# Adding two gated branches: from VectorE to a GpSimd transfer that accumulates

## The reference

```python
y_a = jnp.einsum('bse,ed->bsd', o * jax.nn.silu(r), w_gla_out[l])
u = causal_depthwise_conv(cc * cx, conv_w[l])
y_b = jnp.einsum('bsc,cd->bsd', cb * u, w_conv_out[l])
merged = jax.nn.sigmoid(ga) * y_a + jax.nn.sigmoid(gb) * y_b
x = x + jnp.einsum('bsd,de->bse', merged, w_o[l])
```

## Time and profile before

| | |
|---|---|
| median of 3 runs | 2230.9 us |
| span of the profiled execution | 2229.0 us |
| PE busy | 2217.9 us |
| PEld busy | 1844.9 us |
| DVE busy | 1274.6 us |
| ACT busy | 991.3 us |
| POOL busy | 225.7 us |
| DMA, mean over the span | 200 GB/s |

### The profile page before, as it was taken

How to read it: one execution, slowest core, us unless ns; L and a number is a source line. 1 busy time by engine, 2 the same in 40 slices (tenths; PEclk the granted TensorE clock), 3 DMA queues, 4 the chain that set the end, 5 groups by cost and what they waited for, 6 DMA issues and landing times.

```text
span 2229.0 us, 24387 instructions
## 1 busy us (share of the span) xinstructions
PE 2217.9 (100%) x10314; PEld 1844.9 (83%) x10314; DVE 1274.6 (57%) x1061; ACT 991.3 (44%) x950; POOL 225.7 (10%) x253
## 2 busy tenths in 40 slices
PE   9999999999999999999999999999999999999998
PEld 8888888888888888888888888888888888888886
DVE  6577645545556545555454444554555577786755
ACT  7464654333333443344433433433444455555642
POOL 1023010000000000000000100000100121353201
PEclk9999999999999999999999999999999999999999
DMA  9554556678877766655565555555555756555663
GB/s 321 185 179 162 169 180 199 208 221 224 243 228 231 217 202 199 226 186 191 177 201 188 189 189 189 188 189 189 188 185 194 250 191 196 182 177 176 220 238 117
DMA packets 217100, 444.89 MB, mean 200 GB/s; under 512 B 9316, under 2 KB 10484, under 8 KB 216096
## 3 DMA queue, kind: packets, MB, share of 16 engines
q1 hardware_dynamic: 206976, 411.07, 56.1%
q0 software_dynamic: 9728, 32.18, 6.1%
q10 hardware_dynamic: 288, 0.10, 0.0%
HBM read 427.08 MB, written 12.06 MB: 197 GB/s over the span
## 4 chain that ended last, share of the span: by engine, by line
PE 100%; DVE 0%; POOL 0%; POOLq 0%; ACT 0%; issue 0%
PE acc L1390 31%; PE acc L1391 31%; PE acc L1392 31%; PE side L1400 2%; PE side L1478 1%; PE side L1414 1%; PE side L1450 1%; PE side L1464 1%; PE acc L1405 0%; PE side L1435 0%; PE side L1433 0%; PE side L1434 0%; PE side L1499 0%; PE side L1500 0%; POOL X L657 0%; PE side L1521 0%
## 5 line engine op out<-in xcount | busy, mean ns | idle before, releaser
L954 DVE TENSOR_TENSOR wlo<-raw,whi 128x2048 fp32r<-128x2048 f32 x380 | 892.1, 2348 | 739.3 <-ACT whi L674 739.2
L674 ACT ACTIVATE whi<-raw 128x2048 fp32r<-128x2048 f32 x380 | 727.7, 1915 | 784.9 <-PE acc L1392 762.2
L1390 PE MATMUL acc<-whi,setA_lo 128*128 128x512 f32 x1792 | 700.6, 391 | 0.0
L1392 PE MATMUL acc<-whi,setA_hi 128*128 128x512 f32 x1792 | 697.4, 389 | 0.0
L1391 PE MATMUL acc<-wlo,setA_hi 128*128 128x512 f32 x1792 | 697.4, 389 | 0.0
L1390 PE MATMUL acc<-whi,setB_lo 128*128 128x512 f32 x1280 | 502.9, 393 | 0.0
L1391 PE MATMUL acc<-wlo,setB_hi 128*128 128x512 f32 x1280 | 498.8, 390 | 0.0
L1392 PE MATMUL acc<-whi,setB_hi 128*128 128x512 f32 x1280 | 498.3, 389 | 0.0
L1392 PEld LDWEIGHTS acc<-whi,setA_hi 128*128 128x128 f32 x1792 | 336.4, 188 | 70.1
L1390 PEld LDWEIGHTS acc<-whi,setA_lo 128*128 128x128 f32 x1792 | 336.5, 188 | 69.9 <-DVE setA_lo L985 0.6
L1391 PEld LDWEIGHTS acc<-wlo,setA_hi 128*128 128x128 f32 x1792 | 336.6, 188 | 68.2
(11 more groups left out here) (205 smaller groups left out, 1000.8 us busy)
## 6 DMA issues: line engine op xcount, KB each, us to landing
raw<-in_w_in SPq DMA_DIRECT2D x188, 1024.0 KB, 5.2
raw<-in_w_ffn_up SPq DMA_DIRECT2D x64, 1024.0 KB, 5.3
raw<-in_w_ffn_down SPq DMA_DIRECT2D x64, 1024.0 KB, 5.1
raw<-in_w_gla_out SPq DMA_DIRECT2D x16, 1024.0 KB, 5.2
raw<-in_w_conv_out SPq DMA_DIRECT2D x16, 1024.0 KB, 5.2
raw<-in_w_o SPq DMA_DIRECT2D x16, 1024.0 KB, 5.2
raw<-in_w_out SPq DMA_DIRECT2D x16, 1024.0 KB, 5.2
t_scratch<-t5v POOLq DMA_DIRECT2D x8, 512.0 KB, 7.3
```

Of the source, the lines that this page charges most:

```text
L674: e.activation(whi[r][:, :, :], raw[r][:, :, :], ACT.Copy).then_inc(s_hi, 1)
L954: e.tensor_tensor(wlo[r][:, :, :], raw[r][:, :, :], asf(whi[r][:, :, :]), ALU.subtract).then_inc(s_lo, 1)
L1390: e.matmul(o, xl, whi[r][:, k, :], start=kk == 0, stop=False)
L1392: f = e.matmul(o, xh, whi[r][:, k, :], start=False, stop=kk == 15)
```

## The change

The third DVE instruction of each yb unit goes. In its place POOL, in the same quarter's job "post", waits until the GA part of the unit (unit "ya" j) and the two products are there, and issues one DMA from `GA` (columns of this unit, 128 partitions x 2 x 512 floats, 512 KB) to `tmp` with the accumulate operation add: the transfer reads its destination, adds the source, and writes it back. The transfer raises `s_yb` by 16 when it has landed, and PE waits for 16 (j + 1) in place of j + 1. The whole diff:

```diff
--- before.py
+++ after.py
@@ -619,6 +619,12 @@
                         for i, y in ((1, z1), (2, z2)):
                             e.dma_start(y[i:128, :, :], z[0:128 - i, :, :]).then_inc(s_shift, 16)
                             e.dma_start(y[0:i, 1, :], z[128 - i:128, 0, :]).then_inc(s_shift, 16)
+                    elif job == "post" and UNITS[a][0] == "yb":
+                        j = UNITS[a][1]
+                        e.wait_ge(*evacuated(UI["ya", j]))
+                        e.wait_ge(*evacuated(a))
+                        e.dma_start(tmp_of(a)[:, :, :], GA[:, :, 512 * j:512 * j + 512],
+                                    accum_op=ALU.add).then_inc(s_yb, 16)
                     elif job == "post" and UNITS[a][0] == "up":
                         tm = tmp_of(a)[:, :, :]
                         e.wait_ge(*evacuated(a))
@@ -1086,9 +1092,6 @@
                     e.wait_ge(*tmp_free(u))
                     for t in range(2):
                         e.tensor_tensor(tmp_of(u)[:, t, :], acc[u % 2][t][:, :], GB[:, t, cols], ALU.mult).then_inc(ev, 1)
-                    tm = tmp_of(u)[:, :, :]
-                    e.wait_ge(*evacuated(u))
-                    e.tensor_tensor(tm, tm, GA[:, :, cols], ALU.add).then_inc(s_yb, 1)
                 elif kind in ("wo", "down"):
                     if kind == "wo":
                         e.wait_ge(s_x1, 16)
@@ -1532,7 +1535,7 @@
                         if kind == "r":
                             e.wait_ge(s_rx, 2 * j + 2)
                         elif kind == "yb":
-                            e.wait_ge(s_yb, j + 1)
+                            e.wait_ge(s_yb, 16 * (j + 1))
                         elif kind == "up":
                             e.wait_ge(s_pq, j + 1)
                         else:
```

## The result

| | before | changed |
|---|---|---|
| median of 4 runs, us | 2230.91 (2230.81 to 2230.97) | 2242.91 (2241.24 to 2243.0) |
| span of the profiled execution, us | 2229.0 | 2241.1 |
| the profiled execution's own time, us | not recorded | 2242.88 |

The ratio is 1.0052, with a 95% interval from 1.004 to 1.0064: 12.0 us slower. 2242.3 was forecast.

The account below looks back on a forecast made before the run. TensorE (PE) was taken to bound the kernel, with no slack; three waits of 2.6 us plus one of 3.6 give 11.4, so 2230.9 + 11.4 = 2242.3 us. Range 2232.5 to 2262, the forecast's own 2236 to 2251.

Parts of the forecast that it names:

- That PE's wait is the cost, whole, four times: At the transposes that read tmp, PE waits L - 3.4 us per unit, four times, 11.4 us in all, none regained.
- The removed additions are worth nothing: Four DVE additions, 4.9 us, go; no PE instruction waits for DVE, so the gain is 0.
- The start of the issue, 0.29 us after the products: POOL starts issuing the adding transfer 0.29 us after the second GB product ends, as for the conv stage's shift copy.
- L = 6.0 us: Adding transfer from start of issue to landing: 4.5 copy, 1.3 second read, 0.2 overlap; PE waits 2.6 us per unit.
- +1.0 us in the fourth stage: X1's load pushes weight loads back, so the fourth transfer has half the engines for 2 us: wait 3.6 us.
- The clock at 0: PE's pauses of 2.6 and 3.6 us are shorter than 4.9 us, so the granted clock costs 0.
- The signs named: Wrong if no wait at L1400, landing over 8 us, clock falls, waits for wlo/whi, or waits miss span difference by over 1 us.
- Rival A: The transfer hides: adding costs it nothing, L of 4.5 or less, 4.4 us or less, median 2233 to 2235; chance 0.17.
- rival B: Adding transfer much slower, L of 8.5 or more: 20.4 us, 2251; with clock falls 2255 to 2257; chance 0.23.
- the forecast's own range: Median 2236 to 2251 us, for landing after 4.6 to 8.4 us; chance 0.58.

Follow-up runs that it names:

- the copy: Changed kernel with the four GA-to-tmp transfers as plain copies, without the accumulate operation: 2233.18 us.
- the early load: Changed kernel with the 2 MB load of X1 issued one unit (23 us) earlier: 2242.94 us; second trace 2243.70 us.
- the one-wait kernel: Changed kernel without POOL's wait for the ya part of GA before it issues the adding transfer: 2242.08 us.
- the kernel with half the bytes: Changed kernel with only the first 128 tokens of each unit added by the transfer, the other half by DVE: 2232.39 us.
- the filling: Changed kernel with 16 turns of the identity (1.8 us of PE) put ahead of PE's wait for the sum: 2241.64 us.
- the two filled kernels: Changed kernel with 16 identity turns ahead of PE's wait, without and with X1 loaded one unit earlier: 2241.64 and 2242.21 us.

## Why the prediction was right, point by point

**That PE's wait is the cost, whole, four times.** Shown: with the turns a quarter later the time is that of before; with a second transfer the added wait appears in full.

**The removed additions are worth nothing.** Right. PE's new waits are only the transfers'; and in the kernel with late turns DVE is as much relieved as in the change, at 2230.9.

**The start of the issue, 0.29 us after the products.** Mis-sized: 0.58 measured. The shift copy that I took it from goes through one wait, this one through two; with one it is 0.30.

**L = 6.0 us.** Mis-sized by a little. Measured 5.7, 5.3, 5.5 and 6.6. With the late start, PE's ready time less the start of the issue was 3.1 and not 3.4 us, so the term should have read L - 3.1, and 5.3 to 5.7 gives 2.2 to 2.6 us. The stages were 2.47, 2.05 and 2.32 longer where 2.6 was said. L was put together from 4.5 for a copy and 1.3 for the second stream. Both were off, in opposite directions: the copy of GA lands after 3.5, and the adding is worth 1.9 to 2.1, of which 0.5 is issue. That the three shift transfers queued behind it made the shift copy's 4.4 to 4.6 is likely, but no run parts this from its other shape. The Trainium skill ("Collectives: The Full Stack", section "The bandwidth ceiling: the fold count and why AG ≠ RS ≠ AR") states that a reduce moves at about half the rate of a gather, because it reads two sources. The traces agree roughly: 3.3 us against 1.7 from first packet to last, and 182 and 188 GB/s in slices of the changed kernel where the adding transfer has the engines nearly alone, against 403 for a load. In engine time the adding transfer cost 2.5 times the copy.

```profile
879.00:880.00 1.00, 1.00 (x6) 0.82 (x5) 1.00 (x1) 0.00 (x0) 0.90 (x1) 1.00 1.04 403
...
881.00:882.00 1.00, 1.00 (x6) 0.68 (x4) 0.14 (x1) 0.00 (x0) 0.00 (x0) 1.00 1.09 188
882.00:883.00 1.00, 0.22 (x1) 0.00 (x0) 0.00 (x0) 0.00 (x0) 0.00 (x0) 1.00 1.16 182
```

**+1.0 us in the fourth stage.** 6.6 us in the first trace, about 1.0 above the rest, but the reason given, engines shared with the weight loads that X1 pushed back, explains at most a part. X1's own load had landed at 925.1, 3 us before the transfer's issue. By the trace's semaphore events thirteen of the transfer's 16 completions had come after 5.2 us, as in the other stages, and three came at 5.6, 5.6 and 6.6: single engines were behind, and not all of them. With X1's load in its old place the fourth transfer was late (6.2 to 6.7 us) in five traces of eight, whatever its kind (add, copy, half), and on time (5.3) in three. With the load a unit earlier the third one was late (6.1 and 6.3) in two of three. So the load of X1 seems to have to do with it, but doesn't force it, and one late fourth transfer without it (6.3 us) shows that it is not all. What puts single engines behind stays open.

**The clock at 0.** This step failed. I had read from the end of the span that PE's clock holds for 4.9 us after its last work, and took shorter pauses for safe. That was one pause, seen once. In the first trace of the change a pause of 3.1 us was followed by a fall when PE had already been at work again for 1.0 us. In the four traces of the change and of the early load, pauses of 1.7 to 3.1 us were followed by a fall in 7 cases of 16 (in the change 1 and 2 of four, in the early load 2 and 2); at 0.50 for 3.4 us with PE at work a fall costs 1.6 to 1.7 us. The falls stand behind the longer pauses: seven behind the nine of 2.07 to 3.08 us, none behind the seven of 1.74 to 1.84. The copy had a pause of 2.7 us and the one-wait kernel one of 2.9, both with a fall; the kernel with half the bytes had one of 2.5 us and no fall, and the one with two transfers, with waits of 7.4 to 8.0 us, four falls of four. Waits of up to 1.0 us, with the filling, had none in eight. The runs without a trace point the same way: their mean granted clock is 0.998 or 0.999 in all ten of the two filled kernels, as in the kernel before, and 0.996 or 0.997 in nine of the fourteen of the change, the early load and the one-wait kernel. What decides about the pauses between 2.07 and 3.08 us stays open.

**The signs named.** Two of the signs of being wrong came: the granted clock fell, and PE's new waits, 9.2 us together, miss the difference of the spans, 12.1, by 2.9 where 1 was allowed. Of these 2.9 us 1.7 are the clock and 0.3 lie before the first stage. The other 0.9, some 0.2 a stage, are what a stage is longer than the wait that the view counts; the eight turns themselves take 1.09 us and not 1.03.

The 12.1 us of the spans are thus 10.1 of late sums where 11.4 was said, 1.7 of clock where 0 was said, and 0.3 that comes and goes. The nearness of the total, 0.6 us, is partly luck, since 1.3 too much for the sums and 1.7 too little for the clock nearly cancel. Rival A was right that a lone copy lands sooner, after 3.5 us, and was excluded by what adding costs. That the copy's median, 2233.2, lies in A's 2233 to 2235 is chance: A's own sum at 3.5 us gives 2231.3, and in the copy's trace a late fourth transfer and a fall of the clock make the rest. As for rival B, its price for the clock was due already in the forecast's own range.

## What to carry to other kernels

Where the bound engine never waits, work taken from another engine earns nothing; ask only whether the replacement's result comes before the place where it is read. Here an adding transfer of 512 KB in place of an instruction of 1.2 us brought 0.3 to 0.6 us of start and then 5.3 to 5.7 us to landing, 1.2 of them issue, so it needed some 6 us between producer and reader, and over 7 where it landed late. Moving the reader back one step of the pipeline gave it that for nothing. Price a new pause of TensorE above its own length: the clock may fall behind it, and a pause that can't be avoided may be cheaper filled with idle matmuls (2241.6 against 2242.9 us here, with overlapping intervals).

## What the runs showed of the hardware that I had not expected

- An adding transfer within SBUF, 512 KB: POOL's issue 1.22 us against 0.72 for a copy of the same shape, 5.3 to 5.7 us to landing against 3.4 to 3.6, 3.3 us of all 16 engines against 1.3. For 256 KB: 3.9 to 4.0 us to landing.
- A second wait on a semaphore that was long there put POOL's issue 0.28 us later (0.58 against 0.30).
- The granted clock fell to 0.50 for 3.4 us behind 9 of the 12 pauses of PE of 2.07 to 3.08 us in seven traces, and behind none of up to 1.98 us. Behind waits of 7.4 to 8.0 us it was at 0.50 for 6.8 or 10.2 us.
- POOL's addition with two SBUF inputs stretched DVE's split beside it from 2.28 to 3.94 us.
- A transfer is as late as the last of its 16 completions, and single ones lay 0.4 to 2.7 us behind the rest; where they did, a copy of 3.5 us took 6.2.
